# Loading the first three chunks' expert weights in the out projection, and computing the next layer's first adaLN units behind the experts

## What is computed

```
h  = RMSNorm(x) * (1 + scale1) + shift1            (adaLN from SiLU(cond))
x += gate1 * W_out( sum_b sigmoid(h W_gate + b_gate)_b * Branch_b(h) )
h2 = RMSNorm(x) * (1 + scale2) + shift2
x += gate2 * HierMoE(h2)   (top-1 of 4 groups, then top-2 of 4 SwiGLU experts in the group)
```

```
hid = jnp.einsum('bsd,edf->bsef', h, lp['moe_w1'])
gate, up = jnp.split(hid, 2, axis=-1)
act = jax.nn.silu(gate) * up * dense_w[..., None].astype(h.dtype)
return jnp.einsum('bsef,efd->bsd', act, lp['moe_w2'])
```

## Time and profile before

| what | us |
|---|---|
| median of 3 runs (1853.53 to 1864.29) | 1859.54 |
| the profiled execution: span from first to last instruction | 1860.8 |
| PE busy | 1642.1 (88%) |
| DVE busy | 1196.8 (64%) |
| ACT busy | 888.9 (48%) |
| POOL busy | 435.9 (23%) |
| DMA moved | 351.24 MB, mean 189 GB/s |

### The profile page before, as it was taken

The page is one execution under the profiler, slowest core; times in us unless marked ns, Lnnn a source line. Parts: engine busy times, 40 slices in busy tenths (PEclk is TensorE's granted clock), DMA queues, the critical chain, the costliest instruction groups (busy, mean ns, idle before and its releaser), DMA issues.

```text
span 1860.8 us, 34335 instructions
## 1 busy us (share of the span) xinstructions
PE 1642.1 (88%) x13213; PEld 1100.1 (59%) x13213; DVE 1196.8 (64%) x1888; ACT 888.9 (48%) x1468; POOL 435.9 (23%) x418
## 2 busy tenths in 40 slices
PE   7899889999989986887779998899999999489984
PEld 4578766777765553443466886677776656344443
DVE  5794465777537557777676915477773493687865
ACT  3322545666541124677533235466664311367763
POOL 0132252222241202132203315322222321121302
PEclk8899999999999987998859999999999999799996
DMA  9464246421327476999625632232224454299975
GB/s 334 156 241 136 79 142 214 175 98 61 119 99 258 163 273 220 373 379 364 241 107 178 235 99 90 78 101 75 75 72 130 152 197 179 98 344 379 383 264 191
DMA packets 191250, 351.24 MB, mean 189 GB/s; under 512 B 15493, under 2 KB 98950, under 8 KB 190854
## 3 DMA queue, kind: packets, MB, share of 16 engines
q1 hardware_dynamic: 181791, 320.10, 49.1%
q0 software_dynamic: 7776, 28.32, 4.0%
q10 hardware_dynamic: 1543, 0.88, 0.2%
HBM read 288.24 MB, written 61.01 MB: 188 GB/s over the span
## 4 chain that ended last, share of the span: by engine, by line
PE 61%; DMA 11%; DVE 10%; issue 8%; ACT 5%; DVEq 2%; SPq 1%; POOL 0%; another core or an unknown queue 0%; POOLq 0%; ACTq 0%
PE PS L433 38%; PE PS L440 10%; DMA arena<-in_moe_w 4%; DMA wf<-in_moe_w 4%; PE PS L1079 3%; PE PS L1063 3%; PE PS L865 2%; DVE arena L2404 1%; DMA arena<-in_w_ada 1%; ACT whi L1650 1%; DMA wf<-in_w_in 1%; PE PS L847 1%; ACT arena L1472 1%; DVE xT L2609 1%; ACT arena L1650 1%
## 5 line engine op out<-in xcount | busy, mean ns | idle before, releaser
L1753 POOL TENSOR_TENSOR wlo<-wf,whi 128x256 f16<-128x256 f32 (+1 forms) x268 | 278.1, 1072 | 890.6 <-ACT whi L1399 890.6
L433 PE MATMUL PS<-hpart,whi 128*128 128x320 f16 x2048 | 426.6, 301 | 15.5 <-ACT arena L1472 14.5
L433 PE MATMUL PS<-hpart,wlo 128*128 128x320 f16 x1024 | 308.1, 301 | 0.0
L433 PE MATMUL PS<-whi,hpart 128*128 128x256 f16 (+2 forms) x1568 | 302.2, 293 | 4.8 <-DVE scratch L2024 3.6
L433 PEld LDWEIGHTS PS<-hpart,whi 128*128 128x128 f16 x2048 | 191.5, 98 | 104.6 <-issue 34.9
L433 PE MATMUL PS<-wlo,hpart 128*128 128x256 f16 (+2 forms) x784 | 227.8, 293 | 0.0
L433 PEld LDWEIGHTS PS<-whi,hpart 128*128 128x128 f16 x1568 | 152.9, 99 | 67.1 <-issue 28.2
L2404 DVE TENSOR_TENSOR arena<-arena 128x2048 f16<-128x2048 f32 x66 | 149.5, 2287 | 34.2 <-ACT arena L1650 34.2
L2200 DVE TENSOR_REDUCE stat<-PS 128x1 f32<-128x640 f32 (+1 forms) x160 | 110.7, 713 | 80.3 <-PE PS L1063 78.0
L1472 ACT ACTIVATE arena<-PS,pcol 128x320 f32<-128x320 f32 x128 | 67.4, 527 | 173.5 <-PE PS L433 168.4
L2034 DVE SCALAR_TENSOR_TENSOR scratch<-scratch,cw 128x655 f32<-128x655 f32 x120 | 138.5, 1196 | 4.5
(11 more groups left out here) (349 smaller groups left out, 2782.8 us busy)
## 6 DMA issues: line engine op xcount, KB each, us to landing
arena<-in_moe_w SPq DMA_DIRECT2D x66, 1024.0 KB, 11.2
arena<-in_w_ada SPq DMA_DIRECT2D x40, 1024.0 KB, 8.0
wf<-in_moe_w SPq DMA_DIRECT2D x36, 1024.0 KB, 10.0
wf<-in_w_gate SPq DMA_DIRECT2D x32, 1024.0 KB, 5.5
g_rows<-arena SPq DMA_DIRECT2D x128, 160.0 KB, 1.8
wf<-in_w_in SPq DMA_DIRECT2D x18, 1024.0 KB, 7.4
y_rows<-scratch SPq DMA_DIRECT2D x34, 512.0 KB, 8.7
arena<-g_rows SPq DMA_DIRECT2D x24, 640.0 KB, 5.2
```

The source lines that it names most:

```text
L433: ins = pe.matmul(out, st, mv, start=first and n == 0, stop=last and n == 2)
L1753: ins = pool.tensor_tensor(lo[:, a:b], wf[j][:, a:b], hi[:, a:b], ALU.subtract)
```

## The change

**Experts.** Four pieces, (0,0), (0,1), (0,2) and (1,2), are loaded into the arena as soon as the branch products are done, right behind the last two w_out loads; (1,0) and (1,1) go to the two w_out buffers as these are split; and (2,0), (2,1), (2,2) are loaded as (0,0), (0,1), (0,2) are split. ACT casts (0,0), (0,1), (0,2), (1,0) after the squares 3 to 6 of the out projection, DVE takes the low parts of (0,0), (0,1), (0,2) after the rows 4 to 6, and POOL that of (1,0) in two instructions. Between the first two chunks' rows DVE has (1,1) alone. The buffer sets change places: set 0 is in the arena, set 1's first two pieces are in `wf`. The mixed activations `mhi` and `mlo` lie where `hhi` and `hlo` were. SP then issues (3,0), (3,1), (3,2), (4,0) ahead of the loop, in place of (2,0), (2,1), (3,0), (2,2), (3,1), (3,2), (4,0); the loop is as it was.

**adaLN.** Loads and units 0 to 3 of the second layer leave the out projection and the routing. Loads 0 to 3 follow the last chunks' splits, loads 4 to 7 wait for units 0 and 1, since they reuse their four buffers. PE runs units 0 and 1 after three of the eight band groups, behind a wait for the last chunk's `rows_back`; unit 2 after the eighth; unit 3 after the second tile's `turn_rows_back`. `ada_copy` of unit 2 stands on ACT between the scalings of tiles 0 and 1, that of unit 3 between tiles 1 and 2, `ada_keep` after tile 3's.

```diff
+        mhi, mlo = hhi, hlo
+        mwf = mwa[0:3] + [wf[0][:, :], wf[1][:, :], mwa[3]]
...
-                for j, q in ((0, 2), (1, 0), (1, 1)):
+                for j, q in ((0, 0), (0, 1), (0, 2), (1, 2)):
                     load(slice(j, j + 1), j, q)
-                sp.wait_ge(*w_lo(l, V_ALL))
                 for q in range(2):
-                    load(slice(0, 1), 0, q)
...
+                    sp.wait_ge(*w_lo(l, V_ALL - 1 + q))
+                    load(slice(1, 2), 1, q)
+                for q in range(2):
+                    sp.wait_ge(mw_lo.sem, past * 2 + (q + 1))
+                    load(slice(2, 3), 0, q)
+                sp.wait_ge(mw_lo2.sem, past + 1)
+                load(slice(2, 3), 0, 2)
...
-                        if c and ahead and u >= 2:
-                            ada_unit(l + 1, u - 2)
                 turn_x1(l, KC - 1)
-                if ahead:
-                    ada_unit(l + 1, 2)
...
                 if ahead:
-                    for g in range(8):
+                    for g in range(3):
                         bands(l + 1, g)
+                    pe.wait_ge(my_ready.sem, past + (p * 2 + 6))
+                    for u in range(2):
+                        ada_unit(l + 1, u)
+                    for g in range(3, 8):
+                        bands(l + 1, g)
+                    ada_unit(l + 1, 2)
...
                     if step < TILES:
                         turn_rows_back(step)
+                    if ahead and step == 1:
+                        ada_unit(l + 1, 3)
+                    if ahead and step == 2:
+                        ada_turn(l + 1, 3)
...
                         square(l, k)
+                        if 3 <= k < 6:
+                            part_high(0, 0, 0, k - 3, True)
+                        if k == 6:
+                            part_high(1, 1, 0, 0, True)
...
                         act.mul(cga[:, step, :], cga[:, step, :], rcol[:, 5, step:step + 1]).then_inc(ca_ready.sem, 1)
+                    if ahead and step < 2:
+                        ada_copy(l + 1, step + 2)
+                    if ahead and step == 3:
+                        ada_keep(l + 1, 0)
...
+                pool.wait_ge(mw_hi.sem, past * 3 + 4)
+                pool.wait_ge(mw_lo.sem, past * 2 + 2)
+                for a in range(0, 2048, 1024):
+                    ins = pool.tensor_tensor(mwlo[3][:, a:a + 1024], mwf[3][:, a:a + 1024], mwhi[3][:, a:a + 1024], ALU.subtract)
...
                     rows_kept(k)
+                    if 4 <= k < 7:
+                        part_low(0, k - 4, k - 3)
...
-                part_low(0, 0, 1)
-                part_low(0, 1, 2)
                 rows_low(0, 0)
-                part_low(1, 0, 4)
+                dve.wait_ge(mw_lo.sem, past * 2 + 3)
                 part_low(1, 1, 5)
-                part_low(0, 2, 3)
                 rows_low(1, 1)
```

More of the change, by code:

```diff
@@ L696, in _ @@
                     out_load(u)
-                if ahead:
-                    sp.wait_ge(*g_done(l, HALVES))
-                    for n in range(5):
-                        ada_load(l + 1, n)
                 sp.wait_ge(started.sem, 1)
@@ L783, in _ @@
                     store(p * 2 + (c + 2), c % 2, p * (2 * P) + (c + 2) * P)
+                    if ahead and c == 0:
+                        sp.wait_ge(mw_lo2.sem, past + (p * 2 + 5))
+                        ada_load(l + 1, 3)
                 if ahead:
+                    for n in range(4, PRE):
+                        ada_load(l + 1, n)
                     late_load(l + 1)
@@ L1628, in _ @@
                         high(V_OUT + d - 3, d - 3).then_inc(w_hi.sem, 1)
-                for j in range(2):
-                    act.wait_ge(*y_done(l, 2 * j + 2))
-                    high(V_OUT + 2 + j, j).then_inc(w_hi.sem, 1)
-                    for k in range(3 * j, 3 + 5 * j):
-                        if k == KC - 1:
-                            act.activation(stat[:, 2, 15:16], epsc[:, :], ACT.Sqrt)
-                        square(l, k)
-                        if k in (4, 6) and ahead:
-                            ada_copy(l + 1, k // 2 - 2)
-                act.wait_ge(*total_ready(l, 1))
-                act.activation(stat[:, 0, 0:TILES], total, ACT.Sqrt, bias=epsc[:, :], scale=1.0 / D).then_inc(std_ready.sem, 1)
                 act.wait_ge(started.sem, 1)
@@ L2638, in _ @@
                             in_low(l + 1, step // 2, step % 2 * 1024 + a, step % 2 * 1024 + a + 512)
+                    if l + 1 < LAYERS and step == 4:
+                        modulation(l + 1, 0)
                     if l + 1 == LAYERS and 0 <= step - 2 < TILES:
```

88 lines of the change are left out of this document (36 added, 52 removed).

## The result

The changed kernel takes 1874.0 us (median of 7 runs, 1866.9 to 1879.7), the kernel before 1856.6 (7 runs, 1853.5 to 1864.7). The ratio is 1.0083, with a 95% interval of 1.0056 to 1.011. The kernel has become slower: by 17.4 us between the medians, by 15.4 us by the ratio. The median lies one us above the end of the stated range (1873). Two repeats of the changed kernel (e1, e16) gave 1.0065 (1.0042 to 1.0089) and 1.0074 (1.0041 to 1.0108).

What follows compares the result with a forecast made beforehand. Bounds were taken by stretch: PE in the out projection, DMA in the experts, PE, DVE and ACT in the combine. Terms -5.2 - 2.0 + 0.9 + 4 + 2.2 = -0.1 us gave 1859.4 us, range 1848 to 1873.

Steps and rivals of the forecast that it cites:

- Experts, 0: First chunk's rows onward: earlier loads land into a wait, 0 in both layers, bound -8.3 us a layer.
- My test: Check on the expert stretch: first rows to last result should stay unchanged at 192.8 us.
- To the first rows, -5.2 in layer 1: First gather's issue to first transposes' end: fewer DVE subtractions and one load less ahead, 10.6 to 5.4 us.
- Unit 0 out of PE's loop, -2.0: First layer's out projection: two turns 7.8 us apart instead of 9.7 without the unit, -2.0 us.
- Last turn, +0.9 and +2.2: Out projection's end: DVE's third subtraction delays the last residual; +0.9 us in the first layer, +2.2 in the second.
- The bound of 2.1 us: Out projection's end: added cost a layer if POOL's subtraction goes first and DVE stands still; taken as 0.
- Combine, +4: First layer's combine with four units and turns added: +4 us, between +12.5 at half clock and -5 at full.
- the unexplained waits of 3.8 and 5.9 us: First layer's combine: waits ahead of the last two band adds, taken as room that units would fill without loss.
- the slower combine: Rival: PE at half clock through all units and the untraced wait returning make it 1868 to 1873 us; chance 0.21.
- The unnamed wait: Combine's wait ahead of the last band adds with no cause in the trace; with it, +14 us instead of +8.4.
- Its sign: Slower kernel through the combine is decided once ACT's scaling of tile 2 comes over 10 us after the first `combined`.

Runs made afterwards that it cites:

- e1: Changed kernel repeated with no edit for a second trace; ratio 1.0065 to the kernel before.
- e16: Changed kernel a third time with no edit, on the chip of the thin-unit and small-load variants; ratio 1.0074 to the kernel before.
- e11: Changed kernel with the third chunk's three pieces loaded behind the first gathers, as in the kernel before; ratio 1.0079 to the kernel before.
- e8: Kernel before, with all combine gathers but the first tile's held until DVE's last band add; ratio 1.0013.
- e12: Kernel before, repeated with no edit for a second trace; ratio 1.0000.
- e2: Changed kernel with the low part of (1,0) subtracted by DVE instead of POOL; ratio 1.0059 to the kernel before.
- e7: Changed kernel with (1,0)'s low part on DVE and (0,2)'s subtraction between the last residual and its `rows_kept`; ratio 1.0050 to the kernel before.
- e18: Changed kernel with the second layer's loads 4 to 7 cut to a quarter and units 0 to 3 to two of eight matmuls; ratio 1.0058.
- e17: Changed kernel with the second layer's adaLN loads 4 to 7 cut to a quarter each; ratio 1.0062 to the kernel before.
- the split: Changed kernel with all combine gathers but the first tile's held until DVE's last band add; ratio 1.0129 to the kernel before.
- e14: Changed kernel with the second layer's adaLN loads 4 to 7 cut to a quarter each, on a chip with handfuls; ratio 1.0107.

## Why the prediction was wrong

- **Experts, 0**: right. DMA stands idle ahead of the fourth chunk, and e11 shows that nothing is lost without the third chunk's preload. At equal GB/s both kernels take the same: over the 40 expert stretches of all traces (rates from windows of 120 us, 39 us behind the first rows), those of the kernel before (e8 and e12 included) lie between 0.6 us below and 1.9 above the line through the others. My test, "first rows to last result unchanged at 192.8", was a bad one: it took one trace's length for a constant.
- **To the first rows, -5.2 in layer 1**: right, 10.6 to 5.7 us, and for the reason given. **Unit 0 out of PE's loop, -2.0**: right, 50.3 to 48.4.
- **Last turn, +0.9 and +2.2**: the place and the 2.3 us were right (e2: 7.4 to 7.5, forecast 7.3). Mis-sized was POOL's part. I took 0 because DVE would be ready 0.1 us sooner. It was (1598.52 against 1598.67), but it started only 0.17 us later, most likely because of the register instruction that stands ahead of its subtraction, and POOL started first. The bound of 2.1 us was the value, in both layers (1.9 to 2.0). And one term was missing: behind the wait of 5.5 us the turn runs at half clock, which with what follows costs 1.2 to 1.4 us a layer (e7, where the turn waits 1.26 us and takes 1.53, gives them back). Measured are 2.9 and 4.2 us up to the last turn and about 0.7 and 1.3 behind it, where 3.1 in all was forecast: 6 us too few.
- **Combine, +4**: the step that failed most, by 10 to 11 us. The change costs 14.4 us there in the profiled pair, with handfuls (12.2 and 13.6 if e1 and e16 stand for the changed kernel), and 14.7 in e11 and e12, without. Three parts of it failed. I let the units fill the unexplained waits of 3.8 and 5.9 us. Most likely these were the chip's, since e12 doesn't have them, and where there are handfuls they came again behind the units. I put PE at half clock until 925, at full clock in the middle and at half again in the tiles. It was the other way about: units 0 and 1 ran at full clock (1.92 and 1.93 us in the changed kernel), and then it fell; in e11 and e12 the windows give a PEclk of 0.50 or 0.51 from the second tile on. e18 shows one stretch at the higher level to be worth 3.9 us. And I costed loads 4 to 7 at nothing. The second tile's rows come 5.1 us later, and with a quarter of these loads (e17) `spread` is 2.7 us sooner. The rest, 8.1 us (e18's 51.9 against 43.8), isn't taken apart further; what is left in it is the units' own time, the turns, the copies and the order of bands and units.
- **The rivals**: the slower combine, at 0.21 and 1868 to 1873 us, is nearest to what happened, and part of the match is luck. The unnamed wait did come again, but units 0 and 1 did not run at half clock, and 6 us of the time are from the out projection, outside that rival. Its sign is there in the first trace, where ACT scales tile 2 at 36.2 us, 11.5 after the first combine; in e1 it is 9.9, and in e11, without handfuls, 13.7, so the sign doesn't tell what it was meant to.

By stretches the change is worth -4.9 - 2.0 + 2.9 + 0.7 + 5.5 + 14.5 = +16.7 us, against 15.4 by the ratio and 17.4 between the medians. The Trainium skill (SBUF — State Buffer, "Who interferes with whom") says that a DVE instruction with two inputs in SBUF contends with a POOL instruction that reads SBUF, over ports that are an exclusive lock: whichever is issued first keeps it to its end. The trace agrees: DVE stands still for 1.96 us, POOL's second piece for 2.03. The Trainium skill's rule on code in blocks (Runtime: NRT & Kernel Launch, "Instruction fetch mechanics") would fit handfuls on every engine if blocks came late, but the traces speak against it.

The prediction says that nothing in the trace shows a block's arrival. That is wrong: the DMA view lists queues of the kind "instruction". In the changed kernel q8 moves one packet of 16 KB between 908 and 913 and the next between 928 and 930 (the two lines below, with packets, MB and share of the DMA engines' time), and no instruction queue moves any from 913 to 928, while PE's handfuls run to 923. In e11, without handfuls, they come from 908 to 913 and from 918 to 920. The second comes during unit 2 in both, so it follows PE's program and isn't late.

```profile
q8 instruction: 1, 0.02, 1.4%
...
q8 instruction: 1, 0.02, 3.4%
```

What makes the handfuls, and why only some chips have them, stays open. That POOL's gathers have a part is only argued from the handfuls' end, 2.0 to 2.2 us behind the last gather; whether the split helps on such a chip wasn't tried.

## What to carry to other kernels

Before costing work that is put into a wait, ask for a second trace, if possible from another chip: an unexplained wait may be the chip's, and isn't room. Where two engines may stand in each other's way and start within 0.2 us, take the bound, not the start times. And time a stage between its own events: here the start and the DMA rate moved single traces by 4 and 10 us by chance, where the change moved no stretch but the combine by over 5.

## What the runs showed that I had not expected

- One program has expert stretches from 181 to 194 us at DMA rates of 401 to 367 GB/s; e1 has nearly both ends in one execution.
- Start to first turn is 623.8 to 626.0 or 627.7 to 629.2 us in both kernels. Between 40 and 45 us PEclk is 1.00 in the first trace of before and 0.50 in that of the changed kernel. The five long starts all have 0.50 and a DMA share of 0.54 to 0.68 in that window; the others have 0.50, 0.61 or 1.00, and a share of 0.91 or more:

```profile
40.00:45.00 5.00, 5.00 (x79) 3.07 (x79) 4.72 (x7) 2.48 (x2) 0.00 (x0) 1.00 0.97 313
```

```profile
40.00:45.00 5.00, 5.00 (x29) 3.53 (x30) 4.45 (x7) 1.90 (x1) 0.00 (x0) 0.50 0.57 159
```

- Four 32-column matmuls on different strips take as long as one: both halves of a unit, 512 columns in float32, take 1.90 us at 2.4 GHz and 3.62 at 1.2 GHz, with 8 matmuls (e14, e17) as with 2 (e18).
